# x and mem also loaded with features as rows; quarters for the first two weight chunks; memory loaded later

## The reference

```python
for i in range(DEPTH):                       # DEPTH = 2
    h = rms_norm(x, norm_mix[i])
    if i % 2 == 0:                           # layer 0
        x = x + dsa_moba_mixer(h, positions, ab_w_in, ab_w_out, ...)
    else:                                    # layer 1
        x = x + nsa_mixer(h, positions, nsa_w_in, nsa_w_out, ...)
    x = x + memory_cross_attention(rms_norm(x, norm_mem[i]), rms_norm(mem, norm_mem_src[i]), ...)
    x = x + swiglu(rms_norm(x, norm_ffn[i]), ffn_w_in[i], ffn_w_out[i])

def rms_norm(x, gain):
    y = xf * lax.rsqrt(jnp.mean(xf * xf, axis=-1, keepdims=True) + RMS_EPS)
    return y * gain

def memory_cross_attention(h, m, w_q, w_kv, w_o, q_norm, k_norm):
    q = rms_norm((h @ w_q).reshape(B, S, 4, 128), q_norm)
    k, v = _split(m @ w_kv, (512, 512))
    ...
```

## Time and profile before

| | value |
|---|---|
| median of 3 runs | 1660.69 us |
| profiled execution, span from first to last instruction | 1659.6 us |
| median less that span | 1.1 us |
| PE busy | 1619.1 us, 98% |
| DVE, ACT, POOL busy | 1096.3, 891.3, 421.5 us |
| mean granted TensorE clock | 0.998 |
| HBM read | 262.5 MB, 159 GB/s over the span |

### The profile page before, as it was taken

How to read it: one execution, slowest core, us unless ns; L and a number is a source line. 1 busy time by engine, 2 the same in 40 slices (tenths; PEclk the granted TensorE clock), 3 DMA queues, 4 the chain that set the end, 5 groups by cost and what they waited for, 6 DMA issues and landing times. The chain is left out here.

```text
span 1659.6 us, 26949 instructions
## 1 busy us (share of the span) xinstructions
PE 1619.1 (98%) x10929; PEld 1462.8 (88%) x10929; DVE 1096.3 (66%) x1546; ACT 891.3 (54%) x1401; POOL 421.5 (25%) x460
## 2 busy tenths in 40 slices
PE   8999999999999999999999999999999999999999
PEld 7767899987887889998889998999888999999997
DVE  6875665645576665655577768777646876867763
ACT  6465554434455555443456746566445684756652
POOL 2500100002341120000147802244204690214430
PEclk9999999999999999999999999999999999999999
DMA  7523376556330236665555444766556444376652
GB/s 278 174 77 101 103 205 194 185 197 213 99 135 27 77 102 172 185 186 193 174 195 164 147 133 147 189 185 190 181 154 220 159 153 130 131 204 187 190 179 76
DMA packets 287067, 265.30 MB, mean 160 GB/s; under 512 B 12256, under 2 KB 247520, under 8 KB 286944
## 3 DMA queue, kind: packets, MB, share of 16 engines
q1 hardware_dynamic: 286944, 263.59, 50.8%
HBM read 262.52 MB, written 1.05 MB: 159 GB/s over the span
## 5 line engine op out<-in xcount | busy, mean ns | idle before, releaser
L144 DVE TENSOR_TENSOR w_lo<-w_raw,w_hi 128x2048 fp32r<-128x2048 f32 (+2 forms) x244 | 565.8, 2321 | 288.6 <-ACT w_hi L143 283.6
L143 ACT ACTIVATE w_hi<-w_raw 128x2048 fp32r<-128x2048 f32 (+2 forms) x244 | 462.9, 1902 | 214.6 <-PE bank L529 125.5
L1873 PE MATMUL bank<-h_hi,w_hi 128*128 128x256 f32 x1984 | 565.5, 285 | 4.7 <-issue 1.2
L1874 PE MATMUL bank<-h_lo,w_hi 128*128 128x256 f32 x1984 | 561.3, 283 | 0.0
L1875 PE MATMUL bank<-h_hi,w_lo 128*128 128x256 f32 x1984 | 561.2, 283 | 0.0
L1873 PEld LDWEIGHTS bank<-h_hi,w_hi 128*128 128x128 f32 x1984 | 380.5, 192 | 8.2 <-issue 7.5
L1874 PEld LDWEIGHTS bank<-h_lo,w_hi 128*128 128x128 f32 x1984 | 380.7, 192 | 0.1
L1875 PEld LDWEIGHTS bank<-h_hi,w_lo 128*128 128x128 f32 x1984 | 380.6, 192 | 0.0
L456 PE MATMUL bank<-w_hi,h_hi 128*128 128x512 f32 (+1 forms) x288 | 113.4, 394 | 5.4 <-DVE w_lo L144 3.3
L2953 POOL TENSOR_TENSOR cffn_hidden<-cffn_conv 128x256 f32<-128x256 f32 x44 | 73.7, 1675 | 155.5 <-ACT cffn_conv L2984 155.5
L457 PE MATMUL bank<-w_lo,h_hi 128*128 128x512 f32 (+1 forms) x288 | 111.9, 388 | 0.0
(11 more groups left out here) (447 smaller groups left out, 2858.0 us busy)
## 6 DMA issues: line engine op xcount, KB each, us to landing
w_raw<-in_w_in SPq DMA_DIRECT2D x48, 1024.0 KB, 5.0
w_raw<-in_ffn_w_in SPq DMA_DIRECT2D x88, 512.0 KB, 5.0
w_raw<-in_w_up SPq DMA_DIRECT2D x88, 512.0 KB, 5.2
w_raw<-in_ffn_w_out SPq DMA_DIRECT2D x22, 1024.0 KB, 4.9
w_raw<-in_w_down SPq DMA_DIRECT2D x22, 1024.0 KB, 5.0
w_raw<-in_nsa_w_in SPq DMA_DIRECT2D x10, 1024.0 KB, 5.2
w_raw<-in_mem_w_kv SPq DMA_DIRECT2D x8, 1024.0 KB, 5.1
w_raw<-in_w_branch SPq DMA_DIRECT2D x8, 1024.0 KB, 5.1
```

Of the source, the lines that this page charges most:

```text
L143: return act.activation(hi, raw, ACT.Copy)
L144: return dve.tensor_tensor(self.lo[:, cut_slot, 0:k * n], raw, hi.bitcast(F32), ALU.subtract)
L1873: pe.matmul(out, h, hi[:, f, :], start=(f == 0), stop=False)
L1874: pe.matmul(out, h, lo[:, f, :], start=False, stop=False)
```

## The change

`x` and `mem` are passed a second time, transposed on the host ahead of the launch (`x_cols`, `mem_cols`: 1024 features by 256 tokens). `Features` gets a buffer `cols`. Where it is given, SP loads the features as rows of 1 KB into it in two halves (`load_cols`), ACT and DVE read a feature tile from there and no longer from PSUM, and PE makes no transposes: 16 fewer for x at the start, 16 fewer for mem in layer 0, 16 fewer for mem in layer 1. x as token rows is still loaded, for the squares and the residual, and so is mem, for the squares: each of the three places reads 1 MB more.

`FirstChunk` is made for chunks 0 and 1. Both are loaded in halves and rounded and cut in quarters, with one feature tile ahead of each quarter. x as rows is loaded behind chunk 2, and the squares of x stand behind the rounding of chunk 2 in ACT's list. mem of layer 0 is loaded ahead of chunk 6, and its rounding, squares and cuts are moved from block 0's copies to block 1's, behind the copies of `turn_index`. In layer 0 mem as rows lies in `scaled`.

```diff
-    def load_all(self, sp):
+    def load_all(self, sp, other=None, at=None):
 
         for c in range(self.EARLY, len(self.chunks)):
+            if c == at:
+                other(sp)
             self.wait_cut(sp, self.last_in(self.raw_slot, self.raw_slot(c), c))
             self.load(sp, self.chunks[c], self.raw_slot(c), self.landed[self.raw_slot(c)])
...
+    def load_cols(self, sp, source, half):
+
+        columns = source.rearrange("(f p) q -> p f q", p=P)
+        sp.dma_start(self.cols[:, 4 * half:4 * half + 4, :], columns[:, 4 * half:4 * half + 4, :])\
+          .then_inc(self.cols_in[half], 16)
+
     def view(self, f):
+        if self.cols is not None:
+            return self.cols[:, f, :]
         return self.k.bank[(self.bank + f // 2) % 8][:, (f % 2) * S:(f % 2) * S + S]
...
     def round(self, act, features):
         for f in features:
-            if not self.first:
+            if self.cols is not None:
+                act.wait_ge(self.cols_in[f // 4], 16)
+            elif not self.first:
                 act.wait_ge(self.turned, self.turns[f // 4])
...
     def cut(self, dve, features):
         for f in features:
-            dve.wait_ge(self.hi_done, f - f % 2 + 2 - self.first)
+            dve.wait_ge(self.hi_done, f + 1 if self.cols is not None else f - f % 2 + 2 - self.first)
...
-    def turn(self, pe):
-        pe.wait_ge(self.rows_in, 16)
-        self.features.turn_all(pe)
-
     def load(self, sp):
+        for half in range(2):
+            self.features.load_cols(sp, self.turned, half)
         sp.dma_start(self.rows, self.source.rearrange("(t p) d -> p t d", p=P)).then_inc(self.rows_in, 16)
...
-                self.features.wait_feature(pe, 1 if f == 0 and self.sums[0] == self.bank else f)
+                self.features.wait_feature(pe, f)
...
             @block.sync
             def _(sp):
+                sp.dma_start(k.gains_1[:, :], a["cols_1"]).then_inc(cols_in, 16)
+                for half in range(2):
+                    rows.load_cols(sp, a["x_cols"], half)
+                    first[0].load(sp, half)
+                for part in range(2):
+                    first[1].load(sp, part)
+                w.load(sp, w.chunks[2], w.raw_slot(2), w.early_in[2])
                 sp.dma_start(k.x[:, :, :], a["x"].rearrange("(t p) d -> p t d", p=P)).then_inc(x_in, 16)
-                sp.dma_start(k.gains_1[:, :], a["cols_1"]).then_inc(cols_in, 16)
-                for part in range(2):
-                    first.load(sp, part)
-                for c in range(1, w.EARLY):
-                    w.load(sp, w.chunks[c], w.raw_slot(c), w.early_in[c])
+                w.load(sp, w.chunks[3], w.raw_slot(3), w.early_in[3])
                 sp.dma_start(gain[:, :], row_bcast(a["rows"], 256)).then_inc(gains_in, 16)
                 rope_tables.load(sp)
-                mem.load(sp)
-                w.load_all(sp)
+                w.load_all(sp, mem.load, 6)
...
                 act.wait_ge(cols_in, 16)
-                for i in range(3):
-                    rows.round(act, range(2 * i, 2 * i + 2))
-                    first.round(act, i)
-                first.round(act, 3)
-                rows.round(act, range(6, KD))
-                w.round_to(act, 1)
+                for i in range(KD):
+                    rows.round(act, [i])
+                    first[i // 4].round(act, i % 4)
+                w.round_to(act, 2)
+                act.wait_ge(x_in, 16)
                 for t in range(T):
                     for part in range(2):
                         rows.square(act, t, part)
-                w.round_to(act, 2)
                 rope_tables.act(act)
...
-                    if j == 0:
+                    if j == 1:
+                        turn_index.act(act)
                         mem.features.round(act, range(KD))
                         mem.act_square(act)
-                    if j == 1:
-                        turn_index.act(act)
...
             def _(dve):
-                for i in range(3):
-                    rows.cut(dve, range(2 * i, 2 * i + 2))
-                    first.split(dve, i)
-                first.split(dve, 3)
-                rows.cut(dve, range(6, KD))
-                w.cut_to(dve, 1)
+                for i in range(KD):
+                    rows.cut(dve, [i])
+                    first[i // 4].split(dve, i % 4)
                 rope_tables.dve(dve)
...
-                    if j == 0:
-                        mem.features.cut(dve, range(KD))
                     if j == 1:
                         turn_index.dve(dve)
+                        mem.features.cut(dve, range(KD))
...
-                pe.wait_ge(x_in, 16)
-                rows.turn_all(pe)
-
...
                 def index(pe, j, part):
-                    if (j, part) == (0, 1):
-                        mem.turn(pe)
                     if (j, part) == (1, 1):
-                        pe.wait_ge(mem.features.lo_done, KD)
...
                 pe.wait_ge(project.copied_d, len(blocks))
-                mem.turn(pe)
                 pe.wait_ge(ck_feat, 2)
```

More of the change, by code:

```diff
@@ L207, with __init__ @@
 class FirstChunk:
-    def __init__(self, k, chunk):
-        s, self.w, (self.rows, self.n, sources) = k.sems, k.weights, chunk
+    def __init__(self, k, c, chunk):
+        s, self.c, self.w, (self.rows, self.n, sources) = k.sems, c, k.weights, chunk
         self.source = sources[0][1]
-        self.landed = [self.w.early_in[0], s("first_landed")]
-        self.rounded, self.cut = s("first_rounded"), s("first_cut")
+        self.landed = [self.w.early_in[c], s(f"first_landed{c}")]
+        self.rounded, self.cut = s(f"first_rounded{c}"), s(f"first_cut{c}")
     def load(self, sp, part):
@@ L233, in round @@
         if last:
-            self.w.act_next = 1
+            self.w.act_next = self.c + 1
     def split(self, dve, i):
@@ L251, with __init__ @@
 class Features:
-    def __init__(self, k, name, src, gain, hi, lo, scratch, bank, first=0, stat=None, parts=2):
+    def __init__(self, k, name, src, gain, hi, lo, scratch, bank, first=0, stat=None, parts=2, cols=None):
         s = k.sems
+        self.cols = cols
+        if cols is not None:
+            self.cols_in = [s(f"{name}_cols_in{i}") for i in range(2)]
         self.k, self.src, self.gain, self.hi, self.lo, self.scratch = k, src, gain, hi, lo, scratch
@@ L442, in pe @@
             for c in range(self.first[j], self.last[j] + 1):
-                if c or self.tiles is None:
+                by_tiles = self.tiles is not None and c < len(self.tiles)
+                if not by_tiles:
                     w.wait_cut(pe, c)
@@ L852, in __init__ @@
         gain = k.gains_1[:, (2 + 4 * layer) * KD:(3 + 4 * layer) * KD]
-        self.features = Features(k, "mem_rows", rows, gain, hi, lo, scratch, bank, stat=stat, parts=1)
-        self.bank, self.sums = bank, sums
+        self.features = Features(k, "mem_rows", rows, gain, hi, lo, scratch, None, stat=stat, parts=1, cols=cols)
+        self.sums = sums
     def add_chunks(self, w):
@@ L1121, in block_dsa_moba @@
         gains_in, const = s("gains_in"), s("const")
-        rows = Features(k, "rows", k.x, k.gains_1[:, 0:KD], h_hi, h_lo, k.norm_scratch, 4)
+        x_cols = k.small("x_cols", [P, KD, S])
+        rows = Features(k, "rows", k.x, k.gains_1[:, 0:KD], h_hi, h_lo, k.norm_scratch, None, cols=x_cols[:, :, :])
         after = Features(k, "after", k.x, k.gains_1[:, KD:2 * KD], h_hi, h_lo, k.norm_scratch, 4)
@@ L3062 @@
     arrays = {
-        "x": i["x"][0], "mem": i["mem"][0], "positions": np.ascontiguousarray(i["positions"].reshape(T, P).T),
+        "x": i["x"][0], "mem": i["mem"][0], "x_cols": i["x"][0].T, "mem_cols": i["mem"][0].T,
+        "positions": np.ascontiguousarray(i["positions"].reshape(T, P).T),
         "cols_1": columns(*[v[l] for l in range(2) for v in (i["norm_mix"], i["norm_mem"], i["norm_mem_src"], i["norm_ffn"])],
```

26 lines of the change are left out of this document (13 added, 13 removed).

## The result

The changed kernel takes 1667.54 us (median of 6 runs, 1666.48 to 1668.13), the kernel before 1661.20 (median of 6); the ratio is 1.0038 (95% interval 1.0026 to 1.0050). One run of the kernel before took 3164.51 us; it is among the six, and without it their median is 1660.95. So the change costs 6.3 us by the medians (6.6 without that run), and 5.2 us by the two profiled spans. The forecast was 1665.4, its own range 1663.5 to 1667.5, the whole range 1660.0 to 1668.0. The profiled run of the changed kernel was the shortest of its six (spans 1664.8 to 1666.4).

What follows compares the result with a forecast made beforehand. PE, busy 98% of 1659.6 us, was taken as the bound, with block 1 set by a side chain. Terms +2.7 + 2.0 + 0 + 0 = +4.7 gave span 1664.3, median 1665.4; own range 1663.5 to 1667.5, whole range 1660.0 to 1668.0.

Steps and rivals of the forecast that it cites:

- The chain: Start: later x delays squares, POOL's factors and frequencies, angles, chunk 2's cut and block 1; +2.7 us, range 1.3 to 3.7.
- Rival C: Loads at the start: rows of 1 KB are slow, x lands at 19 to 25; 1668 to 1672 us; chance 0.07.
- D: Start: block 1 does not wait for the chain, earlier block 0 gains up to 3.7 us; 1657; chance 0.07.
- Block 0: Start: PE begins at 8.0, ends at 19.0, 3.7 us earlier, then idles about 9 us; worth nothing.
- The clock: Behind PE's wait before block 1: idleness brings the slow clock back; +2.0 us, bounds 0 and 2.4.
- Rival A: Behind the wait before block 1: clock stays high or recovers at once; 1663.4 us; chance 0.13.
- mem in layer 0: Layer 0: transposes were covered; work moved to block 1's copies leaves chunk 6 0.9 us of cover; term 0.
- mem in layer 1: Layer 1: small scores start 1.97 us earlier, but PE waits for DVE's cut of mem; 0, bounds -2.0 and 0.
- Rival B: Layer 1: removing transposes gains 2.0 us; with chain 1.3 and no clock loss, 1660.0; chance 0.13.
- The quarters of chunk 1: Block 0: finer quarters act only in front of the 9 us wait; term 0.

Runs made afterwards that it cites:

- e1: Changed kernel, but positions loaded behind chunk 0 and POOL writing the rotary frequencies ahead of the factors; 1659.66 us, ratio 0.9992.
- e3: Changed kernel, but x as rows loaded ahead of chunk 2, its squares ahead of chunk 2's rounding, positions loaded behind chunk 0; 1664.60 us, ratio 1.0020.
- e5: Changed kernel, plus 64 PE transposes of the identity behind block 0, during the wait for chunk 2's cut; 1665.38 us, ratio 1.0025.
- e4: Changed kernel, but in layer 1 mem is loaded as rows only and transposed by PE, as in the kernel before; 1666.36 us, ratio 1.0031.
- e10: Kernel before with only the layer-1 part added: mem_cols loaded, no transposes of mem there, cuts from SBUF; 1661.57 us, ratio 1.0005.
- e9: Changed kernel, but layer 1's mem transposed by PE again and 64 identity transposes filling PE's wait behind block 0; 1664.44 us, ratio 1.0020.
- e11: The changed kernel run again without any edit, against the kernel before; 1667.37 us, ratio 1.0037.
- e6: Changed kernel, positions and frequencies earlier, chunk 2 cut before angles, chunk 3 rounded before rotary tables, layer 1's mem transposed by PE; 1657.32 us, ratio 0.9977.
- e2: Changed kernel, but DVE cuts chunk 2 ahead of the rotary angles; 1664.74 us, ratio 1.0022.

## Why the prediction was right, and where it was not

**The chain** (+2.7): right in mechanism and nearly in size. Squares at 17.46 (17.2 forecast), positions landed at 20.8 (21.2), angles at 21.82 (21.6), cut of chunk 2 from 26.03 (25.8), block 1 at 28.37 (28.2). e1 and e3 show that x in the queue sets it and that it goes through to the end. Rivals C and D are out: the rows of 1 KB cost nothing that shows, and the earlier block 0 was worth nothing.

**Block 0**: first product at 8.14 (8.0), end at 20.8 (19.0, or 20 to 21 with a slow start, which it had), idle 7.55 us in place of 9. It cost nothing, as said.

**The clock** (+2.0): right. 1.6 us in the profile, 2.0 to 2.2 by e5. Rival A is out. The granted clock was 0.50 behind 4.83, 6.31 and 7.55 us of idleness, and stayed at 1.00 behind 1.09. The rule of the Trainium skill that the prediction weighed ("TensorE: Matmul & The Clock Gate", Part 1: idleness brings the slow clock back) agrees with these rows. That the size fitted is in part luck: 2.0 was chosen between 1.6 and 2.4 taken from other places, and the traces show 8 to 13 slow steps behind such a wait, 1.6 to 2.6 us.

**mem in layer 0** (0): right. Chunk 6 was cut at 54.5 and PE came to it at 55.2, 0.7 us of cover where 0.9 was forecast.

**mem in layer 1** (0, bounds -2.0 and 0): this is the step that failed. "PE reaches the small scores 1.97 us earlier, and then waits for DVE" put the term at nothing because the start of DVE's cuts did not move; it left out that the cuts themselves take longer when both operands lie in SBUF beside POOL: 4.30 us in place of 3.21. The term is +1.0 us in the profiles and 1.0 to 1.2 by e4, outside its bounds and of the other sign. And the wait did not stand where I put it: PE waited 0.42 us for mem's cut, not 1.5, since the small scores had lost 1.5 us to the lower clock, and 1.54 for the probabilities. Rival B, that the transposes there were worth their time, is out by e4 and e10.

**The sum.** Forecast +4.7; +5.2 by the profiles, where 4.5 (start) and 1.0 (layer 1) are 0.3 more than the whole, most of which PE had regained by 465; +6.3 by the medians, of which 1.1 is layer 1 (e4), 2.1 the clock (e5) and 3.4 the chain (e9). The measured 1667.54 lies 2.1 us above the forecast and just above its own range. The upper bounds of the terms (3.7, 2.4, 0) give 6.1 and so 1666.8; the 1668.0 at which the whole range ended was not worked out from them, and that the time fell inside is luck to that extent. (Rival C's times are also a little off: x landing at 19 to 25 would by its own sum give 1667.2 to 1673.2.) The sum was made for one profiled execution, and the changed kernel's typical run is 0.9 us longer than its profiled one. The cause that I can name is a slow stretch of 3.5 to 5.7 us behind a wait; the runs' granted clocks fit it (e11), but its length in each run is not shown. The three parts make 6.6, within what the medians can tell of 6.3. The quarters of chunk 1 and the later memory of layer 0 have no run of their own; that they cost nothing is read from the traces.

## What to carry to other kernels

Before an input is moved back in a queue, follow who reads it on other engines: here PE got its first operands sooner, and a side chain through ACT, POOL and DVE, all in fixed order, decided when its next block could begin. Here work removed from PE paid only together with the order that let the next weights be cut in time; e6 had both. When an operand moves from PSUM to SBUF, ask what POOL does at that moment.

## What the runs showed of the hardware

- DVE with two SBUF operands beside a POOL instruction that reads SBUF: 534 to 679 ns instead of 476, and POOL 0.63 instead of 0.45 us. With POOL idle the same instruction took 479 ns.
- The slow stretch behind one and the same wait of 7.5 us had 8 steps in two executions and 12 in a third. At the start too: in e2 the first product at 8.08 had the fast pitch at once, in the changed kernel, with the same instructions up to there, the first 7 steps were slow. In e4 the first six products, from 8.17 on, were fast, and then 8 steps were slow, at a granted 0.50 from 10 to 13 us, though PE had no gap there.
- The 32 small scores of 128x32 in layer 1 began at the full clock and fell to 0.50 under way (4.66 to 5.18 us in place of 3.66) when no transposes stood ahead of them; with these ahead, the fall came behind the scores. Whether the small work or the short gaps ahead of it bring the fall was not tried. Transposes of 128x128 without a gap held the clock for 7 us (e5, e9).
